# The recurrence of an RWKV-7 encoder layer laid out anew: whole 128x128 transposes and PSUM bank pairs used in turn

## The reference: what is computed

```
def step(state, inp):
    r_t, w_t, k_t, v_t, an_t, b_t = inp
    sa = einsum('bhij,bhj->bhi', state, an_t)
    state = state * w_t + sa[..., None] * b_t + v_t[..., None] * k_t
    return state, einsum('bhij,bhj->bhi', state, r_t)
```

## Time and profile before

| | |
|---|---|
| profiled execution: span from first to last instruction (no other time is given for it) | 4860.3 us |
| three timed executions, median (range) | 4853.73 us (4845.61 to 4868.58) |
| granted TensorE clock, mean of the execution | 0.935 |
| recurrence: from its first to its last matmul | about 1744 to 2893 us, 1149 us |
| one turn of the recurrence (1149 / 40) | 28.7 us |
| TensorE busy, whole span | 86% |

### The profile page before, as it was taken

The page is one execution under the profiler, slowest core; times in us unless marked ns, Lnnn a source line. Parts: engine busy times, 40 slices in busy tenths (PEclk is TensorE's granted clock), DMA queues, the critical chain, the costliest instruction groups (busy, mean ns, idle before and its releaser), DMA issues. The chain is left out here.

```text
span 4860.3 us, 142503 instructions
## 1 busy us (share of the span) xinstructions
PE 4200.5 (86%) x61166; PEld 3925.7 (81%) x61166; DVE 2967.3 (61%) x5380; ACT 2069.0 (43%) x3696; POOL 1175.3 (24%) x952
## 2 busy tenths in 40 slices
PE   6979999976999967777777769972999999999998
PEld 5869999966888857667667757762999999999998
DVE  6879999945888854444444437757444444444443
ACT  4568888844666621111111112220444444444443
POOL 4544444421444410100011113310111211112110
PEclk9989999967999988999998989985999999999999
DMA  8810000014443331122111226630655655656553
GB/s 168 185 53 23 25 25 23 24 33 146 146 143 133 124 124 56 56 59 66 56 56 56 64 73 180 200 110 28 177 170 172 181 169 178 176 175 173 175 175 104
DMA packets 519591, 542.01 MB, mean 112 GB/s; under 512 B 75200, under 2 KB 456384, under 8 KB 519104
## 3 DMA queue, kind: packets, MB, share of 16 engines
q1 hardware_dynamic: 411840, 425.00, 27.8%
q10 hardware_dynamic: 92480, 62.93, 5.5%
q0 software_dynamic: 14784, 46.57, 4.6%
HBM read 377.99 MB, written 156.43 MB: 110 GB/s over the span
## 5 line engine op out<-in xcount | busy, mean ns | idle before, releaser
L2299 DVE TENSOR_TENSOR g_wlo<-g_raw,g_whi 128x2048 fp32r<-128x2048 f32 x192 | 439.2, 2287 | 115.5 <-ACT g_whi L2261 115.5
L2261 ACT ACTIVATE g_whi<-g_raw 128x2048 fp32r<-128x2048 f32 x192 | 366.4, 1909 | 145.2 <-DMA g_raw<-expert_w_gate 145.2
L2370 PE MATMUL g_pD<-g_whi,g_hh 128*128 128x256 f32 x1536 | 417.2, 285 | 2.5 <-ACT g_o L2288 2.4
L2370 PE MATMUL g_pD<-g_wlo,g_hh 128*128 128x256 f32 x1536 | 408.1, 279 | 0.0
L1119 PE MATMUL c_pP<-c_xh,c_whi 128*128 128x258 f32 x1120 | 329.8, 294 | 35.8 <-DMA c_gup<-g_lora_up 29.5
L1271 POOL TENSOR_TENSOR d_kr<-d_kr,d_fixed 128x512 f32<-128x512 f32 x80 | 104.8, 1316 | 1007.1 <-ACT d_kr L1305 1006.9
L1384 DVE TENSOR_TENSOR d_pm<-d_pP,d_fixed 128x128 f32<-128x128 f32 x400 | 114.1, 290 | 369.9 <-PE d_pP L1441 369.3
L587 DVE TENSOR_TENSOR sapl<-sapT,saph 128x512 fp32r<-128x512 f32 x512 | 329.8, 686 | 2.7 <-ACT saph L546 2.7
L577 DVE TENSOR_REDUCE sanm<-sapS 128x1 f32<-128x1024 f32 x256 | 313.5, 1225 | 26.5 <-PE sapS L628 16.6
L1441 PE MATMUL d_pP<-d_zy,d_br 64*64 64x32 f32 x6400 | 287.3, 227 | 47.1 <-issue 46.9
L1119 PE MATMUL c_pP<-c_xh,c_wlo 128*128 128x258 f32 x1120 | 320.9, 287 | 0.0
(11 more groups left out here) (363 smaller groups left out, 14145.7 us busy)
## 6 DMA issues: line engine op xcount, KB each, us to landing
g_raw<-expert_w_gate SPq DMA_DIRECT2D x64, 1024.0 KB, 5.2
g_raw<-expert_w_up SPq DMA_DIRECT2D x64, 1024.0 KB, 8.4
g_raw<-expert_w_down SPq DMA_DIRECT2D x64, 1024.0 KB, 5.2
ops<-c_ops SPq DMA_DIRECT2D x40, 1024.0 KB, 4.2
d_bd<-ops SPq DMA_DIRECT2D x80, 512.0 KB, 3.9
c_xh<-xT_hi SPq DMA_DIRECT2D x10, 1032.0 KB, 6.1
c_xl<-xT_lo SPq DMA_DIRECT2D x10, 1032.0 KB, 8.7
x_in<-x SPq DMA_DIRECT2D x20, 512.0 KB, 7.5
```

The source lines that it names most:

```text
L2261: act.activation(w_hi[:, Q % NBUF, :, :], raw[:, Q % NRAW, :, :], ACT.Copy).then_inc(s["g_hi"], 1)
L2299: dve.tensor_tensor(w_lo[:, Q % NBUF, :, :], raw[:, Q % NRAW, :, :], w_hi[:, Q % NBUF, :, :].bitcast(F32), ALU.subtract).then_inc(s["g_lo" ...
L2370: mm = pe.matmul(pD[k][:, 0:WB], x[:, d, k * P:(k + 1) * P], w[:, b, d, :], start=(d == 0 and i == 0), stop=(d == DC - 1 and i == len(part ...
```

## The change

In short: (1) each product takes its row half and its column half from (q, a, h), the three bits of the head's number, so that any group of 8 products goes over all four quarter arrays, and row half 0 writes one PSUM bank, row half 1 the other bank of a pair. (2) PSUM is now two pairs of banks a direction: pA (`first`, `second`, `inc`, `left`, `right`) and pB (`grow`, `flipped`). (3) Y is no longer carried: before each level, and once after the last, Z is transposed by two whole 128x128 transposes (`stationary`) and ScalarE copies the result to `Y`. `x4` and `grown_y` fall away. (4) B, K and V are transposed by six whole transposes at the last level (`turned`) in place of 24 small products. (5) Sums over row halves can't be made in PSUM any more: `through` and `out` write two tiles, ScalarE copies one (`known`, `read`) and VectorE adds the other. (6) The order of a turn is new: `join`, then five levels, each with one step of the state between `between` and `grown`. (7) Loads are three DMAs in place of two, and SyncE stores y in four DMAs in place of ScalarE in one.

The core of the diff of TensorE's list, shortened:

```
-            def heads(cross, out, l, r, first=True, last=True):
-                for h in range(2):
-                    mm = pe.matmul(out(halves[1 - h if cross else h]), l(halves[h]), r(halves[h]), start=first, stop=last)
...
+            def at(m, half, x, y):
+                return m[halves[half], 2 * x + y, :]
+            def x12(m, par, g):
+                pe.wait_ge(s[f"d_la{par}{g}"], 16 * (m // 2 + 1))
+                pe.wait_ge(s[f"d_lb{par}{g}"], 32 * (m // 2 + 1))
+                if m:
+                    pe.wait_ge(s["d_bkc"], 2 * (m - 1) + g + 1)
+                for q, a, h in HEADS:
+                    solve(at(left[g], a, h, q), op(par, g, OP_B, q, a, h), both(par, g, q, a, h))
+                    mm = solve(at(right[g], a, h, q), op(par, g, OP_K, q, a, h), both(par, g, q, a, h))
...
+            def turned(m, par, g):
+                pe.wait_ge(s["d_Pe"], 2 * (NL * m + NL - 1) + g + 1)
+                for k in range(2):
+                    for q in range(2):
+                        pe.transpose(left[g][:, 2 * k + q, :], bd[par][g][:, q, (OP_B, OP_K)[k], :, :].rearrange("p a t -> p (a t)"), identf[:])
+                for q in range(2):
+                    mm = pe.transpose(right[g][:, q, :], bv[par][g][:, 2 * q:2 * q + 2, :].rearrange("p a t -> p (a t)"), identf[:])
...
+            def stationary(m, par, l, g):
+                can_use(m, l, g)
+                for h in range(2):
+                    mm = pe.transpose(flipped[g][:, h, :], Z[par][g][:, 2 * h:2 * h + 2, :].rearrange("p q t -> p (q t)"), identf[:])
+                mm.then_inc(s["d_T"], 1)
...
+            def between(m, par, l, g, n):
+                can_between(m, l, g, n)
+                for h in range(2):
+                    for a in range(2):
+                        for q in range(2):
+                            mm = solve(packed(at(inc[g], q, a, h)[:, 0:C // 2], l), at(br[par][g], a, h, q)[:, 0:C], cols(at(Z[par][g], a, h, q), l, g))
...
             def grown(m, par, l, g):
                 pe.wait_ge(s["d_Pe"], 2 * (NL * m + l) + g + 1)
...
+                pe.wait_ge(s["d_Yc"], yc(m, l, g))
+                for h in range(2):
+                    for q in range(2):
+                        for a in range(2):
+                            mm = solve(packed(at(grow[g], a, q, h)[:, 0:C // 2], l), at(Y[par][g], q, h, a), cols(at(pm[l][g], q, a, h), l, g))
...
+            def join(m, par):
+                for g in range(2):
+                    if m < NCH:
+                        x12(m, par, g)
+                    if m:
+                        stationary(m - 1, 1 - par, NL, g)
+                if m < NCH:
+                    for g in range(2):
+                        x3(m, par, g)
+
+            def turn(n):
+                m, par = n + 1, n % 2
+                for l in range(NL):
+                    if m < NCH:
+                        for g in range(2):
+                            stationary(m, 1 - par, l, g)
+                            between(m, 1 - par, l, g, n)
+                    for g in range(2):
+                        if n >= 0:
+                            if l == 0:
+                                through(n, par, g)
+                            if l == 1:
+                                solved(n, par, g)
+                            if l == 2:
+                                out(n, par, g)
+                            if l == 3 and m < NCH:
+                                state(n, par, g)
+                        if m < NCH:
+                            if l == 4:
+                                turned(m, 1 - par, g)
+                            grown(m, 1 - par, l, g)
```

VectorE's part of the new steps:

```
+            def through(n, g):
+                dve.wait_ge(s["d_zkc"], 2 * n + g + 1)
+                dve.tensor_tensor(straight(zs[g][:]), straight(first[g]), turned_over(kv[g][:]), ALU.add).then_inc(s["d_zsc"], 1)
...
+            def out(n, par, i, g):
+                dve.wait_ge(s["d_yac"], 2 * n + g + 1)
+                dve.wait_ge(s[f"d_yst{par}{g}"], 64 * (i + 1))
+                dve.tensor_tensor(straight(y_out[par][g][:]), straight(rs[g][:]), turned_over(second[g]), ALU.add).then_inc(s["d_ye"], 1)
...
+            def turn(n, par, i):
                 for l in range(NL):
                     for g in range(2):
                         between(n + 1, l, g)
...
                     for g in range(2):
+                        if l == 0:
+                            through(n, g)
+                        if l == 2:
+                            out(n, par, i, g)
+                        if l == 3:
+                            state(n, par, g)
                         grown(n + 1, 1 - par, l, g)
```

More of the change, by code:

```diff
@@ L1315, in out @@
[L1315 to L1322, removed]
-                for g in range(2):
[L1324 to L1336, removed]
+                act.activation(tbk[par][g][:].rearrange("p k j t -> p (k j t)").rearrange("p (s c) -> p s c", c=P), left[g], ACT.Copy)
@@ L1348, in _ @@
-            turn(NCH - 1, 1, NCH // 2 - 1, False)
-            for k in ("00", "01", "10", "11"):
-                act.wait_ge(s["d_yst" + k], 16 * (NCH // 2 + 1))
+                    turn(2 * i + par, par)
+                    join(2 * i + par + 2, par)
+            turn(NCH - 2, 0)
+            for g in range(2):
+                stationary(NCH - 1, 1, NL, g)
+            for step in (known, solved, read):
+                for g in range(2):
+                    step(NCH - 1, g)
         @block.vector
@@ L1424, in _ @@
                     grown(0, 0, l, g)
+            begin(1, 1)
             with dve.Fori(0, NCH // 2 - 1) as i:
                 for par in range(2):
-                    turn(2 * i + par, par)
-            turn(NCH - 2, 0)
+                    turn(2 * i + par, par, i)
+                    begin(2 * i + par + 2, par)
+            turn(NCH - 2, 0, NCH // 2 - 1)
             for g in range(2):
-                state(NCH - 1, 1, g)
+                through(NCH - 1, g)
+            for g in range(2):
+                out(NCH - 1, 1, NCH // 2 - 1, g)
         @block.tensor
@@ L1506, in can_begin, with op, both, solve @@
-            def can_begin(m, par, i, g):
-                pe.wait_ge(s[f"d_ld{par}{g}"], 32 * (i + 1))
+            pe.wait_ge(s["d_id"], 2)
+            def op(par, g, k, q, a, h):
+                return bd[par][g][halves[h], q, k, a, :]
+            def both(par, g, q, a, h):
+                return bd[par][g][halves[h], q, OP_A:OP_R + 1, a, :]
+            def at(m, half, x, y):
+                return m[halves[half], 2 * x + y, :]
+            def solve(out, l, r):
+                return pe.matmul(out, l, r, start=True, stop=True)
@@ L1526, in can_between, with can_use @@
+            def can_use(m, l, g):
                 if l == 0:
@@ L1550, in keys @@
[L1550 to L1567 removed]
+                    pe.wait_ge(s["d_Ze"], 2 * (NL * m + l - 1) + g + 1)
@@ new lines, in solved @@
+            def solved(n, par, g):
+                pe.wait_ge(s["d_Yc"], yc(n, NL, g))
+                pe.wait_ge(s["d_zsc"], 2 * n + g + 1)
+                if n + 1 < NCH:
+                    pe.wait_ge(s["d_Pe"], 2 * (NL * (n + 1) + 1) + g + 1)
+                for h in range(2):
+                    for q in range(2):
+                        for a in range(2):
+                            mm = solve(at(first[g], a, q, h), at(Y[par][g], q, h, a), at(zs[g], q, h, a))
+                mm.then_inc(s["d_u"], 1)
@@ new lines, in out @@
+            def out(n, par, g):
+                pe.wait_ge(s["d_uc"], 2 * n + g + 1)
+                if n + 1 < NCH:
+                    pe.wait_ge(s["d_Pe"], 2 * (NL * (n + 1) + 2) + g + 1)
+                for a in range(2):
+                    for h in range(2):
+                        for q in range(2):
+                            solve(at(first[g], q, h, a), at(st[par][g], h, a, q), op(par, g, OP_R, q, a, h))
+                for h in range(2):
+                    for k, (l, r) in enumerate(((uu[g], br[par][g]), (tv[par][g], kr[par][g]))):
+                        for a in range(2):
+                            for q in range(2):
+                                mm = pe.matmul(at(second[g], q, a, h), at(l, a, q, h), at(r, a, h, q)[:, C:], start=(k == 0), stop=(k == 1))
+                mm.then_inc(s["d_yo"], 1)
@@ new lines, in state @@
+            def state(n, par, g):
+                pe.wait_ge(s["d_Pe"], 2 * (NL * (n + 1) + 3) + g + 1)
+                for q in range(2):
+                    for k, r in enumerate((uu[g], tv[par][g])):
+                        for a in range(2):
+                            for h in range(2):
+                                mm = pe.matmul(at(first[g], h, a, q), tbk[par][g][halves[a], k, 2 * q + h, :], at(r, a, q, h), start=(k == 0), stop=(k == 1))
+                mm.then_inc(s["d_sn"], 1)
@@ L1698 @@
+            for n in range(-1, NCH):
+                join(n + 1, (n + 1) % 2)
+                turn(n)
 NE = 16
```

402 lines of the change are left out of this document (135 added, 267 removed).

## The result

| | before | after |
|---|---|---|
| median (range), us | 4861.15 (4845.61 to 4874.25), 4 runs | 4780.77 (4775.91 to 4798.73), 4 runs |
| ratio of the runs, 95% interval | | 0.9854 (0.9825 to 0.9882) |
| the profiled execution: span, mean granted clock | 4860.3 us, 0.935 | 4774.2 us, 0.934 |
| recurrence, first to last matmul | 1738.8 to 2892.4 us, 1154 us | 1715.5 to 2801.9 us, 1086 us |
| one turn, mean of the 39 between the first and the last | 28.6 us | 27.1 us |

By the ratio of the runs the kernel became faster by 1.5%, some 71 us (the two medians are 80 us apart). Forecast were 164. Of the 86 us between the two spans 67 lie in the recurrence.

A forecast was written before the change was run, and what follows sets the result against it. The prediction took TensorE's standing for 256-instruction blocks to bound the recurrence. Cutting a turn from 28.7 to 24.6 us, over 40 turns, took 164 us off 4854, giving 4690 us; range 4590 to 4840.

The forecast's parts named there:

- The bound: Recurrence: TensorE stands for blocks of 256 instructions, 3.92 us each; a turn is 22.4 us running plus 6.3 us standing.
- rival 3: Recurrence: the standing is not the instruction fetch, so 6.3 us a turn stay, 28.1 us; 4830 us, chance 0.06.
- Instructions: TensorE's list in the recurrence: 1876 instructions a turn fall to 1456, 5.69 blocks, about 228 packets in the stage.
- TensorE's own time: TensorE's running time in a turn of the recurrence: products, transposes and shape changes sum to 17.2 us.
- rival 4: Products sharing a row half in turn can't overlap: 28 ns a pair, +7.8 us a turn; 4890 us, chance 0.14.
- A change of shape and back: Array switching between 64*64 and 128*128 around transposes: 28 changes a turn at 0.09 to 0.10 us, 2.7 us.
- the round trip: TensorE to VectorE and back within a level: 0.75 us, taken as covered by other work to within 0.1 us.
- Waits inside a turn: TensorE's waits for VectorE at the join and in the levels: 4.6 us a turn, making running time 21.8 us.
- VectorE's order: In-order VectorE does other work before additions to Z: TensorE waits 0.5 us in level 0, 0.9 and 0.8 in level 3.
- The two together: Each stretch of a turn costs the larger of its running and its fetch; these sum to 24.6 us a turn.
- Rival 2: Longer chain: shape changes at the upper price, +4.3 us, make a turn 27.0 us with stalls; 4786 us, chance 0.13.

The follow-up runs named there:

- e1: Kernel before with 64 tiny products (256 instructions, one block) added to each turn of the recurrence: 5013.72 us, 1.0342 of the kernel before.
- e3: Kernel after without the 24 whole transposes of Z a turn and ScalarE's copies, Y staying zero: 4697.1 us, 0.9702 of the kernel before.
- e7: Kernel after with VectorE's addition to Z put ahead of its through, out and state: 4789.07 us, 0.9863 of the kernel before.
- e6: Kernel after with between and grown streaming all 64 columns in place of the 32 wanted: 4736.78 us, 0.9761 of the kernel before.
- e2: Kernel after with 64 tiny products of one moving column (256 instructions) added a turn: 5023.54 us, 1.0369 of the kernel before.
- e5: Kernel after with 64 products (256 instructions) added a turn, each streaming 64 columns: 4905.99 us, 1.0135 of the kernel before.

## Why the prediction was wrong

The direction was right, and the time lies in the range. The size was wrong: 164 us were forecast, 71 came.

*The bound.* Right. TensorE in the kernel before stands for instruction blocks; e1 shows it with a price of 4.0 us where 3.92 was taken. The trace before shows what it waits for: in the 1020 us from 1760 the gaps recur at every 256th instruction of its list, and where TensorE stood for over 0.5 us at such a border it resumed 1.2 to 1.5 us after a packet of the instruction queue had landed (nine of ten). The rule of the Trainium skill ("Runtime: NRT & Kernel Launch", Instruction fetch mechanics) that dispatch hides the fetch does not hold here, and rival 3 with it.

*Instructions.* Right: 225 packets for 228, and 709 weight loads a turn where the code has 708.

*TensorE's own time.* 14.5 ns a pair: measured 14. So rival 4 is out. The rule of the Trainium skill ("TensorE: Matmul & The Clock Gate", Part 3, The mechanism) from which it would follow does not hold for this order: neighbours that share a row group went at the full pace of four quarters. A change of shape and back was undersized: 0.15 us in (2301.93, the last of 16, to 2302.08), 0.06 more between the first two transposes, 0.09 out, where twice 0.09 to 0.10 was taken; with 14 such pairs some 1.5 us a turn. e3 shows that most of it lies beside the round trip. The Trainium skill ("TensorEngine Tiling (Array Packing)", Key Properties) has the drain without a price.

*Waits inside a turn.* The total of running, 21.8, met the fit's 22.0. e7 bears out that VectorE's order costs 1.4 us of it, e3 that the round trip and not TensorE's work sets most of its length. So the number was right with a wrong division, and that is luck: had TensorE's work been 17.2 of it, e3 would have taken more away.

*The two together.* 24.6 us. At full clock it is right: the seven turns of the trace that ran at 1.00 average 24.8 us, with 2.7 us of standing where 2.8 were forecast. **The step that failed is here**, in what it left out: the sum has no term for the granted clock. The prediction noted 0.92 in the stage and read its prices of TensorE's work at full clock (1.00), without a reason why the rest would cost nothing.

In the kernel before it did cost nothing, because the standing covered it: over its 39 turns a turn's length does not follow its time at half clock (0.01 us per us, standard error 0.07), while its standing shrinks as that time grows (correlation -0.67). Its turns at full clock, only three, average 28.7 us, like all. In the kernel after the same slope is 0.29, standard error 0.04. With the standing cut from 7.6 to 2.7 us the cover is gone, and 6.9 us a turn at half clock cost 6.9 x 0.27 = 1.9 us by the fit, or 27.1 - 24.8 = 2.3 us by the turns at full clock. A turn was forecast at 24.6 us and measured at 27.1, 100 us too long in 40 turns; the missing term is 76 to 92 of these. e6 is the test from the other side: with the half clock cut to 3.1 us the same instructions gave 45 to 57 us back, and its 14 turns at full clock average 25.2 us. Rival 2's 27.0 us has the size by a mechanism that was not there at that price. (In the prediction's chances, the parts named for "faster" come to 0.80, not 0.79; nothing hangs on it.)

*Why the clock fell further* (0.92 to 0.88) is less clear, for TensorE is idle for 4.1 us a turn where it was for 7.2. In both kernels the clock falls after a long stand: just ahead of a fall TensorE stands for 1.9 us (before) or 1.0 us (after) on average, elsewhere at full clock for 0.7 or 0.4. What differs more is how much of a turn is at the lower level: 6.9 us after, 4.7 before. e2 and e5 have the same instructions, waits and places, and granted clocks of 0.66 and 0.87, though e2 is the busier by its rows (1109.66 of 1200 us). So the number of instructions and the busy time alone don't explain the clock. How the chip decides was not settled.

## What to carry to other kernels

Look for a fixed count between TensorE's "issue" gaps: with a list that never repeats and a weight load and matmul every 14 ns, 256 instructions have a price of their own, here about 3.9 us. Two whole transposes in place of eight small products save 28 instructions, by that price 0.43 us, and cost a change of the array's shape and back, 0.3 us where nothing hides it. Before counting a removed stall as gained, ask what time it covered: here a granted clock of 0.92 cost nothing as long as TensorE stood, and the 0.88 after it took about half of the forecast gain once it didn't. Compare stretches with equal work at different granted clock in the kernel before: if they take the same time, something covers the clock, and its price is still to come when the cover is removed.

## What the runs showed of the hardware

TensorE stood at every 256th instruction of a list that is not repeated: 28.6 us for 7.26 blocks in the kernel before, 32.7 for 8.26 in e1. Streaming more columns than wanted made a kernel faster: 32 to 64 columns in 160 of 336 products a turn, half clock from some 7 us down to 3.1, -1% of the whole (e6); in the kernel before, which stood for its blocks, it gave nothing (h9). A change from 64*64 to 128*128 products took 0.15 us and 0.06 us more before the second matmul, the way back 0.09 us. A GpSimd product of 128x512 beside a VectorE addition with both operands in SBUF stretched the latter from 0.42 to 1.04 us.
